# Moving the router of a mixture-of-experts layer beside the projection ahead of it, with 2 MB weight transfers and two norms merged

## The reference, cut to what matters

```python
x = x + memory_cross_attention(h, mem_n, w_q[l], w_k[l], w_v[l], w_o[l])
h = rmsnorm(x, norm_ffn[l])
logits = h @ w_router + b_router          # softmax over the 4 largest of 32
x = x + moe_ffn(h, ...)                   # each expert: (up + 1) * gate * sigmoid(1.702 * gate) @ w_down + b_down
x = rmsnorm(x, norm_final)                # end of the first model, eps 1e-5
for i in range(4):                        # second model, eps 1e-6
    h = rms_norm(x, attn_norm[i])
    x = x + mix_i(h, ...)                 # i = 0: diff_attention, first h @ w_qkv
    x = x + swiglu(rms_norm(x, ffn_norm[i]), f_w_gu[i], f_w_out[i])
```

## Time and profile before

| what | value |
|---|---|
| median of 3 runs | 2766.04 us (2762.4 to 2771.1) |
| the profiled execution: time, span | 2761.77 us, 2759.5 us |
| PE busy | 2642.4 us (96%), 20210 matmul records |
| PEld busy | 2173.7 us (79%) |
| DVE busy | 1433.3 us (52%) |
| ACT busy | 998.1 us (36%) |
| DMA | 663.89 MB on SP's queue, 62.4% of 16 engines, 241 GB/s over the span |
| expert weights | 384 transfers of 1024 KB, 18.1 to 23.0 us from issue to landing |
| dense weights | 241 transfers of 1024 KB, 4.9 us |

### The profile page before, as it was taken

The page is one execution under the profiler, slowest core; times in us unless marked ns, Lnnn a source line. Parts: engine busy times, 40 slices in busy tenths (PEclk is TensorE's granted clock), DMA queues, the critical chain, the costliest instruction groups (busy, mean ns, idle before and its releaser), DMA issues.

```text
span 2759.5 us, 51095 instructions
## 1 busy us (share of the span) xinstructions
PE 2642.4 (96%) x20210; PEld 2173.7 (79%) x20210; DVE 1433.3 (52%) x2698; ACT 998.1 (36%) x1574; POOL 0.2 (0%) x4
## 2 busy tenths in 40 slices
PE   7997999999999999989899999999999999998998
PEld 7996565565555555568899979998899899987998
DVE  5753333333233233257566767666656476665665
ACT  5441121121121211135444465443444344455443
POOL 0000000000000000000000000000000000000000
PEclk9997999999999999999899999999999999999999
DMA  6453999999999999963355434554333255532552
GB/s 249 155 190 133 418 422 422 422 422 422 422 422 422 422 422 422 422 255 108 106 179 184 164 112 146 183 183 140 121 123 125 102 172 183 179 127 92 176 181 102
DMA packets 91895, 665.60 MB, mean 241 GB/s; under 512 B 10208, under 2 KB 10336, under 8 KB 11392
## 3 DMA queue, kind: packets, MB, share of 16 engines
q1 hardware_dynamic: 91776, 663.89, 62.4%
HBM read 662.81 MB, written 1.05 MB: 241 GB/s over the span
## 4 chain that ended last, share of the span: by engine, by line
PE 83%; DVE 6%; DMA 5%; ACT 3%; SPq 2%; issue 1%; DVEq 0%; ACTq 0%
PE bank L268 16%; PE bank L270 15%; PE bank L269 15%; PE bank L2635 14%; PE bank L2652 6%; DMA big<-wdn 5%; PE bank L2623 4%; DVE w_lo L258 2%; SPq L2573 2%; PE bank L2683 2%; ACT w_hi L250 2%; PE bank L2642 1%; PE bank L1133 1%; PE bank L732 1%; PE bank L1141 1%
## 5 line engine op out<-in xcount | busy, mean ns | idle before, releaser
L258 DVE TENSOR_TENSOR w_lo<-ring,w_hi 128x2048 fp32r<-128x2048 f32 (+1 forms) x244 | 557.3, 2284 | 311.5 <-ACT w_hi L250 311.3
L268 PE MATMUL bank<-ht_hi,w_hi 128*128 128x256 f32 x2112 | 611.5, 290 | 3.5 <-DVE w_lo L258 3.1
L270 PE MATMUL bank<-ht_hi,w_lo 128*128 128x256 f32 x2112 | 599.0, 284 | 0.0
L269 PE MATMUL bank<-ht_lo,w_hi 128*128 128x256 f32 x2112 | 598.9, 284 | 0.0
L250 ACT ACTIVATE w_hi<-ring 128x2048 fp32r<-128x2048 f32 (+1 forms) x244 | 464.0, 1902 | 312.7 <-PE bank L270 292.8
L268 PEld LDWEIGHTS bank<-ht_hi,w_hi 128*128 128x128 f32 x2112 | 406.7, 193 | 14.6 <-issue 8.0
L269 PEld LDWEIGHTS bank<-ht_lo,w_hi 128*128 128x128 f32 x2112 | 406.8, 193 | 3.2 <-issue 3.2
L270 PEld LDWEIGHTS bank<-ht_hi,w_lo 128*128 128x128 f32 x2112 | 406.4, 192 | 0.0
L2830 DVE TENSOR_SCALAR big<-bank,big 128x64 f32<-128x64 f32 x256 | 61.0, 280 | 341.5 <-PE bank L2642 341.5
L2635 PE MATMUL bank<-ring,big 128*64 128x256 f32 x2048 | 237.5, 385 | 0.9 <-ACT big L2700 0.9
L2635 PE MATMUL bank<-moe_w,big 128*64 128x256 f32 x2048 | 235.1, 382 | 0.0
(11 more groups left out here) (377 smaller groups left out, 4107.6 us busy)
## 6 DMA issues: line engine op xcount, KB each, us to landing
ring<-post SPq DMA_DIRECT2D x213, 1024.0 KB, 4.9
ring<-wgu SPq DMA_DIRECT2D x128, 1024.0 KB, 18.1
moe_w<-wgu SPq DMA_DIRECT2D x128, 1024.0 KB, 20.1
moe_w<-wdn SPq DMA_DIRECT2D x96, 1024.0 KB, 21.7
big<-wdn SPq DMA_DIRECT2D x32, 1024.0 KB, 23.0
ring<-pre SPq DMA_DIRECT2D x28, 1024.0 KB, 4.9
ring<-post SPq DMA_DIRECT2D x3, 768.0 KB, 4.3
con<-consts SPq DMA_DIRECT2D x1, 1409.5 KB, 13.4
```

The costliest lines, as they stand in the source:

```text
L258: dve.tensor_tensor(w_lo[:, u % SR, 0:w], ring[:, u % R, 0:w], f32(w_hi[:, u % SR, 0:w]), ALU.subtract).then_inc(ph.lo, 1)
L268: pe.matmul(out, wh, xh, start=start and k == k0, stop=False, **kw)
L269: pe.matmul(out, wh, xl, start=False, stop=False, **kw)
L270: mm = pe.matmul(out, wl, xh, start=False, stop=stop and k == k1 - 1, **kw)
```

## The change

Three things. First, the norm stage ahead of the experts is gone. `entry_stage` holds the last part of the w_o projection and the router together: as each of the four tiles is added to `xt`, DVE multiplies two blocks by the gain (`hm`), ACT squares them, and PE transposes them, adds their router products and their squares in bank 4 (`pair`). Pair 0 stands between the halves of tile 2, pair 1 behind tile 2, pairs 2 and 3 behind tile 3. The norm's factor is applied afterwards, to the logits (`scalar_tensor_tensor`) and to the token rows as ACT copies them. The top-k is shorter (ties by one scan), positions are counted from 1, the first expert's selection is taken from them directly and its gather is issued before the item list and the gates are ready, and item 0 is written out ahead of the loop. The down bias is summed in item 0's scatter (8 products more there).

Second, an expert has 6 slots of 2 MB (four for `wgu`, one for each `gate_up`, two for `wdn`) instead of 12 of 1 MB; in HBM the data lie in the order of the slots, 16 KB for each partition, so that one transfer is 128 rows of 16 KB.

Third, the final norm of the first model and the first norm of the second are merged. The `Hand` takes x as it leaves the experts, with the product of both gains. With m the mean square of x and f the final gain, the merged factor is the root of mean(x^2 (f^2 + eps2)) + eps1 eps2, so `reduce` weighs each block's squares by `gain2` (8 dependent instructions). `xt` itself is scaled by the final norm later, inside the first `diff_stage`: `sums`, `final_total`, `final_root`, `final_rstd` and `final_scale`.

The diff, cut (the top-k and the list in their new form are left out, as are the constants):

```diff
-MSLOTS = 12
+MSLOTS = 6
 ...
                 half(pe, 3, 0)
+                if l == 0:
+                    hand.final_total(pe)
                 half(pe, 3, 1)
 ...
                 raw_copy(act, 3)
+                if l == 0:
+                    hand.final_root(act)
                 split_act(act, POST_PH, U + 5)
 ...
                 values(dve, 0)
+                if l == 0:
+                    hand.sums(dve)
                 split_dve(dve, POST_PH, U + 4)
 ...
                 maxes(dve, 1)
+                if l == 0:
+                    hand.final_rstd(dve)
                 split_dve(dve, POST_PH, U + 6)
 ...
                 maxes(dve, 2)
+                if l == 0:
+                    hand.final_scale(dve, 0)
+                    hand.final_scale(dve, 1)
                 split_dve(dve, POST_PH, U + 7)
 ...
                 maxes(dve, 3)
+                if l == 0:
+                    hand.final_scale(dve, 2)
+                    hand.final_scale(dve, 3)
                 split_dve(dve, POST_PH, U + 8)
 ...
-        t = resid_stage("w_o", PRE_PH, pre, PRE["w_o"], None, None, pe_body=out_body)
-        n_ffn = norm_stage("moe", xts, [area(56 + k, 1) for k in range(KB)], ("norm_ffn", 0), D, eps1, after_tiles(t), none)
 ...
         def free_at_start(sp, l):
-            if l < R:
-                sp.wait_ge(pre_lo, N_PRE - R + 1 + (l - N_PRE % R) % R)
-            elif l in (4, 5):
-                sp.wait_ge(pre_done, N_PRE - 1)
-            elif l < 8:
+            if l < 2:
+                sp.wait_ge(pre_lo, N_PRE - 2 * (1 - l))
+            elif l < 4:
                 sp.wait_ge(pre_done, N_PRE)
 ...
-            for l in (10, 11, 8, 9, 0, 1, 2, 3, 4, 5, 6, 7):
+            for l in (5, 4, 0, 1, 2, 3):
 ...
+            def pair(pe, i):
+                pe.wait_ge(s_ehm, i + 1)
+                if i == 0:
+                    pe.wait_ge(s_rtr, 16)
+                for k in (2 * i, 2 * i + 1):
+                    for t_ in range(NT):
+                        mm = pe.transpose(bank[2 * t_ + i // 2][:, (k % 4) * P:(k % 4 + 1) * P], hm[:, k, t_ * P:(t_ + 1) * P], ident)
+                if i % 2:
+                    mm.then_inc(s_ht, 1)
+                for k in (2 * i, 2 * i + 1):
+                    for t_ in range(NT):
+                        pe.matmul(bank[4][:, t_ * E:(t_ + 1) * E], hm[:, k, t_ * P:(t_ + 1) * P], rw[:, k, :], start=(k == 0 and t_ == 0), stop=(k == KB - 1), skip_group_check=True)
+                pe.wait_ge(s_esq, i + 1)
+                for k in (2 * i, 2 * i + 1):
+                    for t_ in range(NT):
+                        mm = pe.matmul(bank[4][:, 2 * E + 2 * t_:2 * E + 2 * t_ + 2], sq[:, k, t_ * P:(t_ + 1) * P], ones[:, 0:2], start=False, stop=(k == KB - 1), skip_group_check=True)
+                if i == 3:
+                    mm.then_inc(s_lg, 1)
+
+            def pe_(pe):
+                out_body(pe, x0)
+                project(pe, PRE_PH, u0 + 2, x0 + 2, "T", o_pairs, between=lambda pe_: pair(pe_, 0))
+                pair(pe, 1)
+                project(pe, PRE_PH, u0 + 3, x0 + 3, "T", o_pairs)
+                pair(pe, 2)
+                pair(pe, 3)
+
+            def act_(act):
+                act.wait_ge(s_hss, hands)
+                for i in range(4):
+                    split_act(act, PRE_PH, u0 + i + SR)
+                    act.wait_ge(s_evac, x0 + i + 1)
+                    act.activation(sq[:, 2 * i:2 * i + 2, :], xt[:, 2 * i:2 * i + 2, :], ACT.Square).then_inc(s_esq, 1)
+                act.wait_ge(s_lg, 1)
+                act.activation(ms_root, bank[4][:, 2 * E:2 * E + 4], ACT.Sqrt, bias=eps1[:, 0:1], scale=1.0 / D).then_inc(s_ert, 1)
 ...
+            def dve_(dve):
+                for i in range(4):
+                    split_dve(dve, PRE_PH, u0 + i + SR)
+                    tile_done(dve, PRE_PH, u0 + i)
+                    o = xt[:, 2 * i:2 * i + 2, :]
+                    dve.tensor_tensor(o, o, blocks(tile_bank(x0 + i)[:, :]), ALU.add).then_inc(s_evac, 1)
+                    dve.wait_ge(s_evac, x0 + i + 1)
+                    dve.tensor_scalar(hm[:, 2 * i, :], xt[:, 2 * i, :], g("norm_ffn", 2 * i), None, ALU.mult)
+                    dve.tensor_scalar(hm[:, 2 * i + 1, :], xt[:, 2 * i + 1, :], g("norm_ffn", 2 * i + 1), None, ALU.mult).then_inc(s_ehm, 1)
 ...
                 pe.wait_ge(m_gue, 4 * i + f + 1)
-                for u in (2 * f, 2 * f + 1):
-                    pe.wait_ge(moe_in[u], 16 * i + 16)
+                pe.wait_ge(moe_in[f], 16 * i + 16)
 ...
+            pe.wait_ge(s_h2, 4)
+            gather(1, list_places)
+            list_codes(pe)
+            turn_gates(pe)
+            item(0, True)
+            pe.wait_ge(s_items, 1)
+            n = pe.value_load(items[0:1, 0:1], min_val=E, max_val=ITEMS - 1)
+            with pe.Fori(1, n) as i:
+                item(i)
 ...
-        first_splits(POST_PH)
-        n_fin = norm_stage("first_final", xts, xts, ("norm_final", 0), D, eps1, moe_stage, none)
+        class TwoNorms(Hand):
+            def reduce(self, dve):
+                dve.wait_ge(s_hsq, 4 * self.j + 4)
+                dve.wait_ge(s_hsum, self.j)
+                dve.sem_inc(s_hadd, 2)
+                link(dve.tensor_scalar(ssq[:, :], sq[:, 0, :], gain2[:, 0:1], None, ALU.mult), dve)
+                for k in range(1, KB):
+                    ins = dve.scalar_tensor_tensor(ssq[:, :], sq[:, k, :], gain2[:, k:k + 1], ssq[:, :], ALU.mult, ALU.add)
 ...
+            def sums(self, dve):
+                link(dve.tensor_tensor(sq[:, 0:4, :], sq[:, 0:4, :], sq[:, 4:8, :], ALU.add), dve)
+                link(dve.tensor_tensor(sq[:, 0:2, :], sq[:, 0:2, :], sq[:, 2:4, :], ALU.add), dve)
+                dve.tensor_tensor(sq[:, 0, :], sq[:, 0, :], sq[:, 1, :], ALU.add).then_inc(s_fsum, 1)
 ...
+            def act_(act):
+                split_act(act, POST_PH, 0)
+                for i in range(4):
+                    hand.hi(act, i)
+                split_act(act, POST_PH, 1)
+                for i in range(4):
+                    hand.square(act, i)
+            def dve_(dve):
+                split_dve(dve, POST_PH, 0)
+                for i in range(4):
+                    hand.lo(dve, i)
+                split_dve(dve, POST_PH, 1)
```

More of the change, by code:

```diff
@@ L52, in const_table @@
     put("before", np.triu(np.ones((P, P)), 1))
-    put("slot", np.tile(np.arange(CAP), (P, 2)))
+    put("slot", np.tile(np.arange(E), (P, 1)))
+    put("slot1", np.tile(1 + np.arange(CAP), (P, 2)))
+    put("level", np.tile(-CAP * np.arange(LEVELS), (P, 1)))
     put("code", (E + np.arange(P))[:, None])
@@ L2074, in program, with gains @@
         INIT = [0.8 - 0.6 * math.exp(-0.3 * i) for i in (0, 3)]
+        def gains(dve):
+            a, f = (par[:, PARAM[n_]:PARAM[n_] + KB] for n_ in ("attn", "norm_final"))
+            dve.tensor_tensor(a, a, f, ALU.mult)
+            link(dve.tensor_tensor(gain2[:, :], f, f, ALU.mult), dve)
+            link(dve.tensor_scalar(gain2[:, :], gain2[:, :], EPS2, None, ALU.add), dve)
         def lam_sums(dve):
@@ new lines, in program, with list_places, list_codes, turn_gates @@
+        entry_stage(out_body)
+        def moe_pe(pe):
+            pe.wait_ge(s_gt, 1)
+            pe.matmul(bank[5][:, 0:E], c("before"), chosen[:, 0, :], start=True, stop=True)
+            pe.matmul(bank[5][:, E:2 * E], ones, chosen[:, 0, :], start=True, stop=False)
+            pe.matmul(bank[5][:, E:2 * E], c("before"), chosen[:, 1, :], start=False, stop=True).then_inc(s_ps, 1)
+            for l in range(LEVELS - 1):
+                for t_ in range(NT):
+                    mm = pe.matmul(bank[7][E * l:E * (l + 1), 0:2], chosen[:, t_, :], ones[:, 0:2], start=(t_ == 0), stop=(t_ == 1))
+            mm.then_inc(s_cn, 1)
+            def list_places(pe):
+                pe.wait_ge(s_il, 1)
+                pe.matmul(bank[7][0:NC, 4:6], c("before")[0:NC, 0:NC], over[0:NC, 0:2], start=True, stop=True).then_inc(s_ps, 1)
+            def list_codes(pe):
+                pe.wait_ge(s_il, 2)
+                pe.matmul(bank[7][0:1, 16:32], c("code")[0:NC, 0:1], over[0:NC, 8:24], start=True, stop=True)
+                pe.matmul(bank[7][0:1, 32:48], c("expert")[0:NC, 0:1], over[0:NC, 8:24], start=True, stop=True)
+                pe.matmul(bank[7][0:1, 48:50], over[0:NC, 0:1], ones[0:NC, 0:2], start=True, stop=True).then_inc(s_ps, 1)
+            def turn_gates(pe):
+                pe.wait_ge(s_gt, 2)
+                for t_ in range(NT):
+                    mm = pe.transpose(bank[0][0:E, t_ * P:(t_ + 1) * P], gates[:, t_, :], ident)
+                mm.then_inc(s_gtp, 1)
+            def gather(value, between=None):
@@ L2620, in gather @@
                 pe.wait_ge(m_sel, value)
                 for d in range(KB):
+                    if between is not None and d == KB // 2:
+                        between(pe)
                     for t_ in range(NT):
@@ L2713, in moe_act @@
             rows(0)
+            act.wait_ge(s_gtp, 1)
```

(30 more changed lines are left out.)

249 lines of the change are left out of this document (114 added, 135 removed).

## The result

| | before | after |
|---|---|---|
| median (lowest to highest) | 2766.5 us (2762.4 to 2771.1) | 2740.8 us (2740.0 to 2740.9) |
| profiled execution: time, span | 2761.8, 2759.5 | 2740.7, 2738.9 |
| first expert's products begin | 263.26 | 239.32 |
| MoE end (end of the last scatter) | 1203.94 | 1188.01 |
| from there to the end of the span | 1555.6 | 1550.9 |

The changed kernel is faster: ratio 0.9906, 95% interval 0.9889 to 0.9923, 25.7 us between the medians. Between the two profiled executions it is 21.1, since before's lies 4.7 under its median. 2733 was forecast and the range, 2720 to 2752, holds the time; of the 32.7 us 7 are missing by the medians and 11.6 by the traces. The traces say where.

The account below looks back on a forecast made before the run. PE was taken to bound twenty experts (29.09 us each), then DMA the last (29.84). Experts' end -26.1 and exit net -6.6 make -32.7 us, off the median 2766.0: 2733 us, range 2720 to 2752.

Parts of the forecast that it names:

- Entry: From w_o's last tiles to the first expert: its products begin at 240.0 instead of 263.3, 23.3 us earlier.
- rival C: PE keeps the high clock through entry and exit: 5.7 and 1.8 us less, 2726 us; chance 0.1.
- Item 0: First expert: the down-bias product comes back there at full clock, 7.2 / 2 = 3.6 us on PE.
- 2 MB transfers: Expert loop: PE stays at 29.09 us per expert, DMA goes from 29.84 to 29.58 and holds the end at 1177.8.
- per byte: Expert loop: if the stream's extra 0.087 us per MB is paid by bytes, DMA stays at 29.84 us per expert.
- per transfer or per packet: Expert loop: if the extra is paid so, halving their number gives 0.52 us per expert, 29.32, and PE holds the end.
- Rival A: Expert loop: DMA's time goes by bytes alone, 29.84 us per expert, end at 1185.6, 2741 us; chance 0.25.
- Rival D: Weight loads: 16 KB packets move worse, 0.9 us each, 43 us per expert, 3155 us; chance 0.05.
- MoE end: End of the expert loop: 1177.8 against 1203.9, 26.1 us earlier, with DMA holding it.
- Exit: From the experts to the first a_qkv unit: 10.6 us less, net 6.6 after what the final norm gives back.
- The final norm gives back: In the a_qkv stage: wait for sums 1.7, product 0.6, scalings 2 and 3 1.7, together 4.0 us on the path.
- Rival B: A_qkv stage: what left the exit returns whole, 8.6 us on the path, 2738 us; chance 0.1.

Follow-up runs that it names:

- bias_full: Changed kernel with down biases and gates zero-padded to 128 rows, and item 0's bias products all ahead of its scatter products: 2728.3 us.
- whole_8k: Changed kernel with each 2 MB slot still loaded by one transfer, but weights laid out in HBM in rows of 8 KB: 2747.8 us.
- half_loads: Changed kernel with each 2 MB slot loaded by two transfers of 1 MB, in rows of 8 KB: 2752.3 us.
- old_exit: Changed kernel with the earlier kernel's separate final norm stage and handover put back, and no final norm steps in the a_qkv stage: 2749.1 us.
- norm_moved: Changed kernel with the final norm's product over the sums, reciprocal and scalings placed later in the a_qkv stage: 2738.0 us.
- half_rows: Changed kernel with each 2 MB slot loaded by two 1 MB transfers cut by partitions (64 and 64), rows still 16 KB: 3633 us.

## Why the prediction was right or wrong

- **Entry: right.** First products at 240.0 forecast, 239.3 measured (-23.9 us instead of -23.3). Logits 225.5 (226.1), selection 228.7 (228.6), first gather at 231.2. The scans, taken at 0.5 us each for want of a row, take 0.23. The gather ran at half clock as rows 7 had let expect, so rival C did not come true here.
- **Item 0: the step that failed.** The forecast took before's 7.2 us for the bias products at the low clock and halved it, 3.6. The price per product was right: it is what 128-row products cost in bias_full, and 32-row ones at full clock take about as long. Two things were not asked: what the products stand between, and what they do to the clock. Alternating with the scatter they made 16.1 us of 2.0, and the fall of the clock 1.8 more behind: 15.9 instead of 3.6, 12.3 us too little in the sum. Rows 4 and 7 held a weak hint: those same 32-row products ran at 0.50 for 7 us with PE busy; so, though, did the 128-row gather behind them.
- **2 MB transfers: right in kind, a size off.** The middle, 29.58, was taken between "per byte" (29.84) and "per transfer or per packet" (29.32); measured is 29.37, so nearly all of it is per packet, and not per transfer (whole_8k). PE's 29.09 became 29.07. With it DMA did not hold the end (1177.8 forecast as the later of the two); PE did. Rival A, 29.84 us per expert to the end, is what half_loads and whole_8k show with 8 KB rows; after, with 16 KB rows, does not. Its time, 2741, meets the measured 2740.8, nearer than the forecast's 2733: that is a coincidence, and by the number alone the wrong mechanism would have been chosen. Rival D, 16 KB packets worse, is refuted: 0.62 us per packet, two of 8 KB less 9 ns (which is how the 9 ns were found), not 0.9; the instruction fetches were a bad yardstick.
- **MoE end.** Forecast -26.1, measured -15.9: entry -23.9, item 0 +15.9, waits for DMA gone -7.4, and 32 x 0.02 = -0.6 of the period, together -16.0. The gap of 10.2 is item 0's 12.3, less 2.1 by which the entry (0.6), the period (0.6) and DMA, which no longer held the end (0.9), did better than forecast. That the time still lies in the range is luck in this sense: the range was made wide for A and for unseen steps, and no rival had item 0's cost in it.
- **Exit: right.** The first a_qkv unit is done 11.4 us behind the MoE end, before 22.2: -10.8 (forecast -10.6). The final norm gives back 4.2 by the first `turn_out` (1261.89 against 1284.45, 22.6 earlier, where the first unit was 26.8 earlier; forecast 4.0): 1.74 of wait, the product of 0.7, and 1.68 for scalings 2 and 3, which are on the chain. Net -6.6; old_exit has 6.8 and the forecast -6.6. Rival B falls. The terms are less exact than their sum: norm_moved got only 1.2 of the 1.7 of wait back.
- **Behind the exit.** From the MoE end to the end of the span it is only 4.7 us shorter than before, not 6.6. Up to the last `times_v` it is 8.3 shorter (129.2 against 137.5), and from there to the end 3.6 longer (1421.7 against 1418.1; half_loads has 1417.0). Windows of the latent stage, 400 to 420 us behind the MoE end, after and then half_loads:

```profile
1588.00:1598.00 10.00, 7.18 (x49) 5.41 (x48) 5.68 (x12) 7.29 (x16) 0.00 (x0) 0.90 0.29 105
1598.00:1608.00 10.00, 10.00 (x63) 7.15 (x62) 4.18 (x12) 2.67 (x10) 0.00 (x0) 0.76 0.32 107
```

```profile
1598.70:1608.70 10.00, 7.18 (x59) 6.09 (x59) 5.90 (x13) 7.07 (x16) 0.00 (x0) 1.00 0.30 105
1608.70:1618.70 10.00, 10.00 (x80) 7.87 (x81) 7.03 (x16) 3.96 (x13) 0.00 (x0) 1.00 0.32 107
```

PE is busy for 7.18 and 10.00 us in both, and the code is the same; in after the clock falls, in half_loads and in before it does not, and half_loads needs 2.0 us less from the MoE end on. A second fall of this kind stands in after some 990 us behind the MoE end (0.85 over 20 us), where before has 0.95 and half_loads 0.97. All other runs show the first fall too, half_rows aside, old_exit among them. half_loads is the changed kernel but for its transfers, so it is nothing that the change put there; that it hangs on when the stretch comes is an inference, and was not tried.

## What to carry to other kernels

A product that is added inside an existing group is not priced by its own duration: ask whether it breaks up products that ran beside each other on separate rows, and whether it has fewer rows than they. Put products of one row count in a block and pad a 32-row one, best so that two halves can run side by side; here that turned 17.9 us (16.1, and 1.8 behind) into 3.7. That this holds beyond these 32-row fp32 products of 256 columns is not shown. Where PE and DMA have nearly the same period, a gain of 1.5% in the transfer rate moves the bound: compare both periods and the lead, not the busy shares.

## What the runs showed of the hardware that was not expected

- The granted clock fell to 0.50 under a PE that was busy without a gap, during products over 32 rows (in all eight traces that have them in item 0), and stayed at 1.00 during the same number of records over 128 rows or over two halves of 64.
- Alternating 32-row and 64-row products: 0.31 us per record of 256 fp32 columns at full clock, against some 0.22 for the 32-row ones, 0.23 for 128-row ones and 0.12 for the 64-row ones in blocks of their own.
- Weight rows of 16 KB move at 428 GB/s and rows of 8 KB at 422, whether in transfers of 1 or 2 MB.
- Transfers that write 64 of the 128 partitions, one half after the other, move at 214 GB/s, half of the rate, while all 16 DMA engines are shown busy.
- The same stretch with the same idle time of PE ran at clock 1.00 in one kernel and at 0.77 in another; such places differ from kernel to kernel, and the kernels compared here differ by 2 to 4 us of the whole with them.
